# Moving the copies of the scan's solved values from VectorE to ScalarE in a DeltaNet + PEER layer kernel

## The reference, cut to what matters

```python
v_new = u_i - jnp.einsum('bhck,bhkv->bhcv', w_i, s)
s_next = s * jnp.exp(gl_i)[..., None, None] + jnp.einsum('bhck,bhcv->bhkv', kd_i, v_new)
o_i = jnp.einsum('bhck,bhkv->bhcv', qd_i, s) + jnp.einsum('bhij,bhjv->bhiv', a_i, v_new)
```

## Time and profile before

| what | value |
|---|---|
| median of 3 timed runs | 2041.45 us (2038.69 to 2042.62) |
| the profiled execution | 2037.75 us, span 2035.9 us |
| mean granted TensorE clock | 0.993 of full speed |
| PE busy | 1968.3 us, 97% of the span |
| DVE busy | 1493.3 us, 73% |
| POOL busy | 1043.5 us, 51% |
| ACT busy | 948.6 us, 47% |

### The profile page before, as it was taken

How to read it: one execution, slowest core, us unless ns; L and a number is a source line. 1 busy time by engine, 2 the same in 40 slices (tenths; PEclk the granted TensorE clock), 3 DMA queues, 4 the chain that set the end, 5 groups by cost and what they waited for, 6 DMA issues and landing times.

```text
span 2035.9 us, 36049 instructions
## 1 busy us (share of the span) xinstructions
PE 1968.3 (97%) x12502; PEld 1753.5 (86%) x12502; DVE 1493.3 (73%) x3430; ACT 948.6 (47%) x1695; POOL 1043.5 (51%) x657
## 2 busy tenths in 40 slices
PE   5799999999999998999999999999999999999997
PEld 2688888888878878889999999999998888888886
DVE  4788888888421146779889677777468888888888
ACT  3555555445342235334334578888533333333332
POOL 0346555665334475447899776666763222222222
PEclk9899999999999999999999999999999999999999
DMA  7323223332222363335888799999999999999993
GB/s 275 116 79 110 89 100 110 110 105 83 68 93 94 124 207 130 106 106 168 274 284 270 251 314 360 361 366 367 395 359 373 361 379 353 360 348 352 365 346 120
DMA packets 151777, 469.93 MB, mean 231 GB/s; under 512 B 15632, under 2 KB 46576, under 8 KB 148464
## 3 DMA queue, kind: packets, MB, share of 16 engines
q1 hardware_dynamic: 108064, 300.13, 42.1%
q0 software_dynamic: 36864, 134.23, 18.1%
q10 hardware_dynamic: 6736, 34.08, 4.2%
HBM read 415.38 MB, written 53.00 MB: 230 GB/s over the span
## 4 chain that ended last, share of the span: by engine, by line
PE 87%; DVE 6%; POOL 2%; issue 1%; ACT 1%; DMA 1%; SPq 1%; POOLq 0%; ACTq 0%; DVEq 0%
PE bank L2978 25%; PE bank L607 14%; PE bank L609 14%; PE bank L608 14%; PE bank L2965 4%; POOL w_lo L1288 2%; PE pair L607 2%; PE pair L609 1%; PE pair L608 1%; DVE cv L1617 1%; PE bank L2577 1%; PE bank L2567 1%; PE pair L2629 1%; PE bank L2910 1%; DMA ada_c<-w_ada 1%
## 5 line engine op out<-in xcount | busy, mean ns | idle before, releaser
L1288 POOL TENSOR_TENSOR w_lo<-raw,w_hi 128x1024 fp32r<-128x1024 f32 x148 | 362.2, 2451 | 391.8 <-ACT w_hi L808 171.8
L607 PE MATMUL bank<-lat_hi,w_hi 128*128 128x384 f32 (+2 forms) x1488 | 535.8, 360 | 4.2 <-DVE lat_lo L2080 2.6
L609 PE MATMUL bank<-lat_hi,w_lo 128*128 128x384 f32 (+2 forms) x1488 | 521.5, 350 | 0.0
L608 PE MATMUL bank<-lat_lo,w_hi 128*128 128x384 f32 (+2 forms) x1488 | 521.0, 350 | 0.0
L1441 POOL DMA_INDIRECT rows<-peer_v,e_row x128 | 136.7, 1068 | 337.3 <-DVE pair L2298 317.3
L607 PEld LDWEIGHTS bank<-lat_hi,w_hi 128*128 128x128 f32 x1488 | 281.3, 189 | 18.2 <-issue 4.5
L609 PEld LDWEIGHTS bank<-lat_hi,w_lo 128*128 128x128 f32 x1488 | 280.5, 189 | 17.9
L608 PEld LDWEIGHTS bank<-lat_lo,w_hi 128*128 128x128 f32 x1488 | 281.2, 189 | 13.4 <-issue 0.2
L1288 POOL TENSOR_TENSOR w_lo<-raw_more,w_hi 128x1024 fp32r<-128x1024 f32 x80 | 199.8, 2500 | 92.7 <-ACT w_hi L1025 64.2
L2978 PE MATMUL bank<-w_lo,c_hi 128*128 128x512 f32 x768 | 237.1, 389 | 0.0
L2978 PE MATMUL bank<-w_hi,c_lo 128*128 128x512 f32 x768 | 237.1, 389 | 0.0
(11 more groups left out here) (403 smaller groups left out, 3581.2 us busy)
## 6 DMA issues: line engine op xcount, KB each, us to landing
raw<-w SPq DMA_DIRECT2D x210, 512.0 KB
raw_more<-w SPq DMA_DIRECT2D x142, 512.0 KB
g_dram<-gs ACTq DMA_DIRECT2D x24, 1024.0 KB
gu_dram<-gu SPq DMA_DIRECT2D x120, 192.0 KB
gq<-g_dram SPq DMA_DIRECT2D x45, 512.0 KB
gl<-gu_dram SPq DMA_DIRECT2D x28, 768.0 KB
ada<-w_ada SPq DMA_DIRECT2D x32, 512.0 KB, 3.4
dY<-gc_dram SPq DMA_DIRECT2D x8, 768.0 KB, 4.2
```

The costliest lines, as they stand in the source:

```text
L607: nc.tensor.matmul(out, hi, rh, start=start, stop=False)
L608: nc.tensor.matmul(out, hi, rl, start=False, stop=False)
L609: return nc.tensor.matmul(out, lo, rh, start=False, stop=stop)
L1288: nc.gpsimd.tensor_sub(w_lo[:, slot, :], raw_at(slot % 2 if src is None else src), w_hi[:, slot, :].bitcast(F32)).then_inc(split_done, 1)
```

## The change

ACT gets the copies into `Vn` in the heads 0 to 6, at a fixed place of its order for each step; DVE keeps them in head 7 alone. It is 12 copies of 128x128 a head, 84 in all. The semaphores are the same, with the waiting engine changed.

```diff
+            def new_values(h, s):
+
+                for d in range(NDIR):
+                    act.wait_ge(solve, h * 12 + (2 * s + d + 1))
+                    nc.scalar.copy(Vn[:, d, :], bank[3 + d][:, 0:P]).then_inc(vn, 1)
+
             def next_head(h):
 
                 n = h + 1
                 middle_tap(n, K_LAT)
+                new_values(h, 0)
                 weigh_part(h, 2)
                 exp_decay(n, range(0, 6))
+                new_values(h, 1)
                 middle_tap(n, K_CTX)
                 weigh_part(h, 3)
                 exp_decay(n, range(6, NU))
+                new_values(h, 2)
                 act.wait_ge(kd_done, n * 3)
...
                 silu_of(n, K_LAT)
                 middle_tap(n, V_LAT)
                 silu_of(n, K_CTX)
+                new_values(h, 3)
                 next_hi(n, 0)
                 middle_tap(n, V_CTX)
                 act.wait_ge(turned, n * 4)
                 silu_of(n, V_LAT)
+                new_values(h, 4)
                 silu_of(n, V_CTX)
                 next_hi(n, 1)
                 silu_z(n, 5)
+                new_values(h, 5)
                 next_hi(n, 2)
...
-            def new_values(h, s, d):
+            def last_new_values(h, s, d):
...
-                    for d in range(NDIR):
-                        new_values(h, s, d)
+                    if not more:
+                        for d in range(NDIR):
+                            last_new_values(h, s, d)
```

## The result

The changed kernel takes 2054.14 us (median, 2050.70 to 2055.67), the kernel before 2041.02 in the same comparison: a ratio of 1.0064, 95% interval 1.0049 to 1.0079. It is slower by 13.1 us, more than the 5.5 forecast and just outside the range (2052.8). The profiled execution took 2052.96 us, its span 2051.1. That is 15.2 us more than the profiled execution before, which had been a quick one, 3.3 us under its median; so the profiles show somewhat more than the medians do.

A forecast was written before the change was run, and what follows sets the result against it. PE, running in order, was taken to bound the changed heads. Delays of 1.0 us in the first and 0.75 in six others, 5.5 us, added to the 2041.45 median gave 2046.95, stated as 2047.0; range 2040.5 to 2052.8 us.

The forecast's parts named there:

- What bounds the kernel: Seven changed heads: PE bounds them, busy 381.01 of 392.16 us; freeing DVE wins at most PE's 5.5 us of waits.
- The cast behind step 3's solves: Step 3 on ACT: cast 1.92 us later, shifting POOL's additions past 1.25 us of slack, so PE loads row late.
- Win and loss cancel: Step 3: PE's 0.35 us lateness mostly vanishes in its 0.3 us wait for DVE, leaving the solve 0.1 us late.
- Step 1: Copies behind six exponentials on ACT: first done at about 237.3, making PE at most 0.1 us later.
- the 0.75: PE's delay in us at row in step 4 of the third head, repeated in the heads after it.
- The sum: Seven heads: first head 1.0 us late, six others 0.75 us each, 5.5 us in all.
- likeliest case: Whole kernel, time range of the main forecast: stated as 2045.2 to 2048.2 us.
- The copy itself: One 128x128 copy from PSUM on ACT: 271 ns, from a straight line through the times of wider tiles.
- The first rival: Sum chain stays hidden, cast shifted by less than 1.25 us of slack: no measurable change, 2042.5 us; chance 0.18.
- the second: Rival: DVE's relief reaches the solves, 13 waits and 5.5 us go: 2036.0 us; chance of faster 0.12.
- The third rival: Step 4: rk and kdr both collide with POOL's additions, Rd 1.5 us late, 11 us in all: 2052.6; chance 0.15.
- the main case: Step 4: rk slips behind POOL's second addition, kdr behind the third, Rd at about its old time; chance 0.55.

The follow-up runs named there:

- e5: Changed kernel with ACT's copies of step 0 ahead of the middle tap, step 1 behind four of six exponentials, step 3 behind the cast: 2040.40 us.
- e6: Changed kernel with the copies of steps 0 and 1 back on DVE and step 3's behind the cast: 2040.16 us.
- e1: Changed kernel with step 3's copies behind the cast of the weight tile instead of in front of it: 2041.92 us.
- e4: Changed kernel with PE's sum_columns behind the two projection blocks of slot 1 in step 4 instead of in front: 2042.08 us.
- e2: Kernel before, all copies on DVE, with ACT waiting for both solves of step 3 ahead of the cast: 2051.41 us.
- e3: Changed kernel with three unused 128x512 products a head issued by PE ahead of its wait for row in step 4: 2045.58 us.
- e10: e5 with two of POOL's four additions moved ahead of its weight tile: 2032.69 us.
- e7: Changed kernel unaltered, run again: 2053.37 us, ratio 1.0064 against the kernel before.
- e8: Kernel before, copies on DVE, with two of POOL's four additions moved ahead of its weight tile: 2033.12 us, ratio 0.9970.

## Why the prediction was wrong

- **What bounds the kernel, and that the copies stand on no chain:** right. Step 4's wait stayed at 0.66 us in the changed kernel, and no placing of the copies brought the third head below the 56.01 us of before (e5, e6).
- **The cast behind step 3's solves, POOL's chain behind it, PE late at `row`:** right in mechanism and place. Cast at 16.28 us into the head (forecast 15.9), additions ending at 25.09 (24.8), PE 1.12 us late (0.75). Confirmed by taking it away (e1, e4) and by bringing it in alone (e2).
- **"Win and loss cancel: I put the solve of step 3 at +0.1":** wrong in size, +0.47 (251.62 - 236.29 = 15.33 against 14.86). PE's lateness out of steps 0 and 1 was put at 0.35 us and was 0.55 when it came to step 2's product; the part put too low is "Step 1: at most 0.1 more", where the load waited 0.40 us for `Vn` (242.79). And DVE's second state waits for a second product that PE issues 0.44 us after the first; the 0.26 us distance before was DVE's own backlog. It starts 12.75 us into the head against 12.28:

```profile
248.60 0.35 DVE L1850 SCALAR_TENSOR_TENSOR St<-St,egl,pair 128x128 f32<-128x128 f32 x1 [0.43 <-PE pair L2648]
249.04 0.35 DVE L1850 SCALAR_TENSOR_TENSOR St<-St,egl,bank 128x128 f32<-128x128 f32 x1
```

This is the 0.37 us by which the 0.75 was short in six heads, 2.2 us in all. The first head, put at 1.0, had its weight load 1.16 us late.
- **"The sum. 1.0 + 6 x 0.75 = 5.5 us":** the step that failed. It counted PE's delay as the length of its pause and took the clock for granted, though the rows had the granted clock beside them, 1.00 in the head shown. What the clock would cost was thus put at nothing. The pause for `row` came just behind the 0.66 us wait for `Rd`, and behind the two the granted clock was at half for 3.4 us in five of seven heads, 1.55 us each, 7.8 us. e3 shows it: with the pause filled the first six heads all take 56.9 to 57.2 us, as the two short ones had. (A slip beside it: by its own terms the likeliest case starts at 2045.4, not 2045.2.)
- **The copy itself,** priced at 271 ns, took 0.25 to 0.28 us.
- **The first rival** (hidden) did not come, and **the second** (both waits of DVE go) could not: e5 takes away the lateness of steps 0 and 1 and of the cast, e10 also POOL's hold on `rk`, and neither gains anything from DVE's relief.
- **The third rival** (double collision, 2052.6) came close to the time by chance and is not what happened. DVE in the changed kernel:

```profile
258.55 0.17 DVE L1667 TENSOR_SCALAR rk<-rk 128x6 f32<-128x6 f32 x1
...
258.98 1.08 DVE L1673 TENSOR_TENSOR kdr<-kds,r 128x12 f32<-128x12 f32 x1
259.99 0.34 DVE L1835 SCALAR_TENSOR_TENSOR Rd<-pair,nexp,Vt 128x128 f32<-128x128 f32 x1
```

`rk` slips in between POOL's second and third addition, `kdr` waits for the third: the main case as described. `Rd` of step 4 comes 23.70 us into the head against 23.22, 0.48 us later, which is the 0.47 of step 3.

What stays open is why two of seven heads keep the clock with the same pause; the runs show only that which ones differs from execution to execution.

## What to carry to other kernels

Moving work to an idle engine moves its waits with it: a copy that must wait for its producer makes everything behind it in that engine's order late, here a cast whose result fed a chain of POOL, whose slack of 1.25 us was smaller than the shift. Work out the slack of each consumer of what is queued behind the moved instruction before counting what the other engine saves. And when PE is the bound, look for existing pauses next to a new one: here a new pause of 0.40 us just behind one of 0.66 was followed in five of seven heads by a fall of the granted clock that cost 1.55 us more. Look at what PE did just ahead, and fill the pause or move the request behind work that is ready.

## What the runs showed of the hardware

- Two waits of PE, 0.66 and 0.40 us, with little work between them were followed by half of the granted clock (0.50) for 3.4 us in five of seven heads, in both profiles of the changed kernel, and so were 0.59 and 0.40 us in e2. The first wait alone was followed by none: 0.66 us in the kernel before, up to 0.80 in e6. Three products of 128x512 whose results nobody uses, in the place of the second wait, prevented it in the first six heads and the one of step 4 in the seventh, and the kernel became 7.8 us faster for them (e3 against e7).
- `rk`, a DVE operation on 128x6 values, takes 0.17 us when no addition of POOL stands in its way, and 1.08 to 1.20 us when one is running, until that addition ends; `kdr` (128x12) takes 0.17 and 1.08. e8, which only moves POOL's additions away, turns 1.08 into 0.17 and wins 6.6 us. The reciprocal between the two took 0.19 us also at 258.76 in the changed kernel, inside POOL's run of additions (256.01 to 261.38). The Trainium skill ("SBUF — State Buffer", section "SBUF: two separate sides") describes an exclusive lock on a port pair that is held for the whole instruction. For `rk` (one input and a constant) and for `kdr` (two inputs), whichever meets the addition, the trace agrees. It does not show a hold behind every POOL instruction: in e8 `kdr` took 0.17 us at 249.51, while POOL's `invr` is listed from 249.41 for 1.33 us.
